# A transformer block on one core: the gate projection spread over the first attention steps, and the last two heads' values behind the first output block

## The chip, the cores and the metric

The kernel runs on one core of a Trainium2 chip. The metric is the device time of one execution in microseconds (us); lower is better. The engines named here are TensorE (PE in the profile), ScalarE (ACT), VectorE (DVE), GpSimd (POOL) and SyncE (SP), whose queue issues the weight loads.

## The reference, cut to what matters

Two transformer blocks run one after the other on 256 tokens of width 1024. The change is in the first one, in its token mixer, between the two feed-forward layers:

```python
h = _rms_norm(x, mix_norm[layer])
proj = h @ w_in[layer]
aq, ak, av, hq, hf, hi, hg = jnp.split(proj, split_at, axis=-1)
...
attn_out = _dilated_attention(aq, ak, av).astype(x.dtype).reshape(b, s, ATTN_WIDTH)
rec = _hgrn2(hq.reshape(b, s, HG_HEADS, HG_EXPAND), hf.reshape(b, s, HG_HEADS, HG_EXPAND),
             hi.reshape(b, s, HG_HEADS, HG_VDIM), lower_bounds[layer]).astype(x.dtype)
rec = _rms_norm(rec, hg_out_norm[layer]) * jax.nn.silu(hg.reshape(b, s, HG_HEADS, HG_VDIM))
mixed = jnp.concatenate([attn_out, rec.reshape(b, s, HG_WIDTH)], axis=-1)
x = x + mixed @ w_out[layer]
```

There are eight attention heads of 64 channels and a chunked linear recurrence of four heads of 128 channels, in chunks of 64 tokens. The gate `hg` is used only at the end: its silu multiplies the normalised output of the recurrence. The value `av` is used from the first head's probabilities on.

## The kernel before, in words

**Weights.** All weights come in blocks of 128 x 2048 floats. A list `plan` gives their order; `sp_stream` loads them into a ring of eight places as places come free. Products are made to float32 precision from halves: `act_split` (L293) has ACT round a block to its high half (the copy at L299), `dve_split` (L302) has DVE subtract it to get the low half (L307), and each product is three matmuls (high by high, high by low, low by high). A high half has one of four places, so block n is split only after block n-4 is used up on PE. A block is held by both engines in the order of their own programs: each `act_split(..., index + SPLIT)` written between other work splits the blocks up to four ahead.

**Order.** Every engine has a program of its own, written out by hand, which runs strictly in order; semaphores join them. PE's program for the mixer is `pe_mix` (L733), ACT's is `act_mix` (L768), DVE's is `dve_mix` (L875). All matmuls are issued by `mm` (L178).

**Projections.** `pe_tok` (L528) multiplies the tokens by a 1024 x 512 weight: two blocks (halves of the contraction), each 24 matmuls of 512 columns, into two PSUM banks (one for each 128 tokens). The blocks are `w_tok` 0 and 1 (q and k), 3 (`hi`), 4 (the gate `hg`) and 2 (`av`), used in this order. Between the two halves of `w_tok` 4 stand the recurrence's first products of heads 0 and 1 (`pe_rec_head`, with transposes at L649), after it those of heads 2 and 3 and the turning of q (`pe_qk_turn`, L699); between the halves of `w_tok` 2 stand the first chunk state (`pe_rec_state`) and the turning of k. ACT empties the banks with `kept` (L797): copies for `hi` and `av`, silu for the gate into `SHG`.

**Attention steps.** Then comes a loop over 11 steps. Step i holds on PE the scores of head i (`pe_scores`, two matmuls with 64 rows of weights), the transposes of head i-2's probabilities (`pe_turn_p`, L720) and the values of head i-3 (`pe_pv`, three matmuls). Steps 0 and 1 also hold the chunk states 1 and 2, step 4 the recurrence's outputs (`pe_rec_out`, 20 products). On DVE a step is the bias and minimum (`biased`, L922 and L924), the scaling by the reciprocal sum (`scaled`, L930 to L933) and, in odd steps from 5 on, the low half of two heads' values (`values`, L938); on ACT two exponentials (`exps`, L808 and L810), the copy of the transposed probabilities (`turned_p`, L817) and the high half of the values (L821). ACT takes the squares of the recurrence's outputs in step 6 (`squares`, L832, eight of them) and their roots in step 8 (L838); DVE makes the means in step 7 (`means`) and the gated product in step 9 (`gated`, L971). `states` (L956) carries the chunk states forward on DVE.

**Output.** Four blocks of `w_out` follow (`pe_down`, 24 matmuls each) into banks 2 to 5: block 0 needs heads 0 to 3, block 1 heads 4 to 7, blocks 2 and 3 the recurrence, whose gated outputs `pe_rec_turn` (L684) transposes between blocks 0 and 1 and `rec_xt` (L843 on ACT) writes back. The next stage is the residual addition and the norm before the second feed-forward layer, and then that layer.

## Time and profile before

| what | us |
|---|---|
| median of three runs | 1333.2 |
| lowest and highest of the three | 1331.91 and 1340.69 |
| the profiled execution, its own time | 1335.28 |
| its span in the trace | 1333.4 |
| busy time of PE over the span, and its share | 1269.5 (95%) |
| busy time of DVE and of ACT | 612.2 (46%) and 466.9 (35%) |
| the token mixer with its output blocks, in the trace | about 214 to 347 |

The page gives for each engine the time in which it was busy, as a share of the span. In the timeline a row is a run of like instructions: its start, the time from the first one's start to the last one's end, the engine, line and operation, how many, and in brackets how long the engine stood idle before it and what released it. The ends of matmuls are modelled and overlap the next one's start, so the time of PE work is best read from start to start. A float32 matmul that isn't made from halves is two instructions in the trace, a transpose is one.

### The profile page before, as it was taken

What the parts mean: (1) busy time and instruction counts of PE and PEld (TensorE: products, weight loads), DVE (VectorE), ACT (ScalarE), POOL (GpSimd) and SP (SyncE); (2) the same over time, 40 slices, a digit from 0 to 9 for tenths busy, and PEclk for the clock granted to TensorE, in tenths of its full rate; (3) what the DMA queues carried; (4) which work ended last, traced back from release to release, by engine and by line L of the source; (5) the groups of instructions that cost most, each with busy time, mean ns of one, the idle gap of its engine ahead of it and who ended that gap; (6) DMA issues with size and microseconds to landing.
All of it is one profiled execution on the core that took longest, in us unless ns stands there. A gap on an engine that the chain in (4) does not pass through costs nothing.

```text
span 1333.4 us, 18498 instructions
## 1 busy us (share of the span) xinstructions
PE 1269.5 (95%) x7906; PEld 924.0 (69%) x7906; DVE 612.2 (46%) x816; ACT 466.9 (35%) x634; POOL 205.6 (15%) x207
## 2 busy tenths in 40 slices
PE   6999999998999999999899999997999899999995
PEld 6999997886799999888664444434898665444432
DVE  6644556845676764476731111117465651111114
ACT  5544344655446444325410101014676420001111
POOL 0000000410499990030000000000033000000000
PEclk9999999999999999989999999998999999999998
DMA  9555553540555555515599999996523399999992
GB/s 390 185 180 180 186 190 129 191 159 28 174 185 187 190 189 167 190 41 188 200 373 419 422 421 420 421 421 248 169 92 127 127 350 395 421 421 421 421 420 113
DMA packets 47750, 338.33 MB, mean 254 GB/s; under 512 B 5296, under 2 KB 5296, under 8 KB 7728
## 3 DMA queue, kind: packets, MB, share of 16 engines
q1 hardware_dynamic: 45936, 330.53, 64.6%
q10 hardware_dynamic: 1728, 6.55, 1.3%
q8 instruction: 66, 1.08, 0.3%
q14 instruction: 20, 0.16, 0.0%
HBM read 336.02 MB, written 1.05 MB: 253 GB/s over the span
## 4 chain that ended last, share of the span: by engine, by line
PE 89%; DVE 7%; ACT 2%; issue 1%; DMA 1%; SPq 0%; ACTq 0%; DVEq 0%
PE pb L178 88%; DVE halves L307 1%; DVE SM L1476 1%; DVE Xs L1487 1%; DMA ring<-in_ffn_w 1%; PE pb L1916 1%; DVE Xs L403 0%; DVE Xs L1482 0%; DVE Xs L405 0%; DVE XN L340 0%; ACT halves L299 0%; DVE p L1655 0%; DVE XN L349 0%; DVE Xs L1500 0%; DVE XTl L392 0%
## 5 line engine op out<-in xcount | busy, mean ns | idle before, releaser
L178 PE MATMUL pb<-XTh,halves 128*128 128x256 f32 x1856 | 338.8, 283 | 6.9 <-DVE XTl L392 4.9
L307 DVE TENSOR_TENSOR halves<-ring,halves 128x2048 fp32r<-128x2048 f32 (+1 forms) x122 | 285.1, 2352 | 130.2 <-ACT halves L299 129.9
L178 PEld LDWEIGHTS pb<-XTh,halves 128*128 128x128 f32 x1856 | 291.2, 192 | 9.1 <-issue 4.1
L178 PE MATMUL pb<-XTl,halves 128*128 128x256 f32 x928 | 262.3, 283 | 0.0
L299 ACT CAST halves<-ring 128x2048 fp32r<-128x2048 f32 (+1 forms) x122 | 227.4, 1874 | 83.4 <-PE pb L178 79.4
L178 PE MATMUL pb<-ring,gather 128*64 128x512 f32 x832 | 189.8, 598 | 3.2 <-DVE gather L2054 1.7
L178 PEld LDWEIGHTS pb<-XTl,halves 128*128 128x128 f32 x928 | 177.8, 192 | 0.9
L178 PE MATMUL pb<-halves,XTh 128*128 128x512 f32 x512 | 160.5, 395 | 5.0 <-DVE halves L307 3.0
L178 PEld LDWEIGHTS pb<-ring,gather 128*64 128x64 f32 x832 | 57.5, 137 | 109.2 <-issue 105.0
L2050 DVE TENSOR_TENSOR slots_h<-slots_silu,pb 128x256 f32<-128x256 f32 x32 | 13.5, 421 | 229.3 <-ACT slots_silu L2012 229.3
L178 PEld LDWEIGHTS pb<-halves,XTh 128*128 128x128 f32 x512 | 95.6, 190 | 26.0 <-DVE halves L307 6.0
L178 PE MATMUL pb<-halves,HTh 128*128 128x512 f32 x352 | 110.8, 396 | 0.0
L178 PE MATMUL pb<-halves,XTl 128*128 128x512 f32 x256 | 100.0, 391 | 0.0
L2058 DVE SCALAR_TENSOR_TENSOR slots_y<-pb,SM,slots_y 128x512 fp32r<-128x512 f32 x32 | 24.0, 751 | 117.4 <-ACT slots_y L2024 117.4
L178 PEld LDWEIGHTS pb<-places,XN 128*128 128x128 f32 x512 | 60.1, 193 | 23.4 <-issue 23.4
L1679 POOL TENSOR_TENSOR p<-p,CO 128x256 f32<-128x256 f32 x16 | 14.9, 959 | 392.1 <-DVE p L1659 392.1
L2024 ACT ACTIVATE slots_y<-pb,SM 128x512 fp32r<-128x512 f32 x32 | 22.0, 688 | 152.2 <-PE pb L178 152.2
L178 PEld LDWEIGHTS pb<-halves,HTh 128*128 128x128 f32 x352 | 64.8, 188 | 14.1
L178 PE MATMUL pb<-ring,slots_ht 128*64 128x512 f32 x320 | 72.9, 597 | 0.0
L178 PE MATMUL pb<-halves,HTl 128*128 128x512 f32 x176 | 69.6, 395 | 0.0
L178 PE MATMUL pb<-places,XN 128*128 128x128 f32 x512 | 65.8, 283 | 1.6 <-ACT gate_sig L1840 1.6
L2016 ACT COPY slots_ht<-pb 128x256 f32<-128x256 f32 x32 | 11.9, 372 | 138.4 <-PE pb L1916 138.0
(348 smaller groups left out, 1389.4 us busy)
## 6 DMA issues: line engine op xcount, KB each, us to landing
ring<-in_moe_w SPq DMA_DIRECT2D x144, 1024.0 KB, 13.6
ring<-in_ffn_w SPq DMA_DIRECT2D x66, 1024.0 KB, 5.0
extra<-in_moe_w SPq DMA_DIRECT2D x48, 1024.0 KB, 14.6
ring<-in_w_tok SPq DMA_DIRECT2D x10, 1024.0 KB, 5.0
ring<-in_ple_gate SPq DMA_DIRECT2D x8, 1024.0 KB, 4.9
ring<-in_w_out SPq DMA_DIRECT2D x4, 1024.0 KB, 4.9
ring<-in_ab_out SPq DMA_DIRECT2D x4, 1024.0 KB, 4.9
ring<-in_sb_v SPq DMA_DIRECT2D x4, 1024.0 KB, 22.8
```

Of the source, the lines that this page charges most:

```text
L178: return e.matmul(out, l, r, start=start, stop=stop, **kw)
L299: e.copy(split_of(n)[0], raw_of(n)).then_inc(*high.mark(n))
L307: e.tensor_tensor(l, raw_of(n), h.bitcast(F32), ALU.subtract).then_inc(*low.mark(n))
L1476: s = e.bn_stats(st4[:, t, h, :], X3[:, t, h * 512:h * 512 + 512])
L1487: e.scalar_tensor_tensor(x, x, r, GB[:, 1024:2048], ALU.mult, ALU.add).then_inc(*x_new.mark("norm", i, t))
L1679: e.tensor_tensor(diag(LL[h % 8]), diag(LL[h % 8]), strict2, ALU.mult).then_inc(*sb_strict.mark(h))
L1916: j = e.transpose(banks[7][:, c * 128:c * 128 + 128], HM[n][:, c * 128:c * 128 + 128], ident)
L2016: e.copy(HT4[p % 2][:, 2 * n:2 * n + 2, :], banks[7][:, 0:256]).then_inc(*s.h_kept.mark(p, n))
L2024: e.activation(Y[h][0], down_bank(p, h)[:, :], ACT.Copy, scale=slot_gate[:, p:p + 1]).then_inc(*s.y_high.mark(p, h))
L2050: e.tensor_tensor(HM[n], SL[n], banks[5 + n][:, 256:512], ALU.mult).then_inc(*s.mul.mark(p, n))
L2058: e.scalar_tensor_tensor(Y[h][1], down_bank(p, h)[:, :], slot_gate[:, p:p + 1], Y[h][0].bitcast(F32), ALU.mult, ALU.subtract).then_inc(*s. ...
```

## The change

The gate's projection (`w_tok` 4) changes places with that of the values (`w_tok` 2), in the plan and in `pe_mix`: values go first, to banks 4 and 5, with the products of heads 0 and 1 and the turning of q between the halves. q is turned into banks 2 and 3 as k is. A new function `pe_gate` issues the gate's 48 matmuls in four pieces, to banks 6 and 7: 8 ahead of state 0, then 13, 13 and 14 at the end of the PE work of steps 0, 1 and 2 (in step 2 ahead of the transposes). The chunk states 1 and 2 move from steps 0 and 1 to steps 1 and 2, and the recurrence's outputs from step 4 to step 3. The values of head 0 and 2 now wait until ACT has emptied banks 6 and 7.

ACT takes the gate's silu, one split and the first four squares in step 3, the last four squares in step 8 and the roots in step 10; a split moves to before step 0 and one to step 1. DVE has splits in steps 0, 1 and 3, and the means and the gated product in steps 9 and 10. The values of heads 6 and 7 move behind output block 0, whose first write to each bank now waits for the last reader of that bank.

```diff
--- before.py
+++ after.py
@@ -209,7 +209,7 @@
         plan_ffn("ffn1", a["ffn1_w13"], a["ffn1_w2"], GROUPS)
         plan_all("w_hf", a["w_hf"])
         plan_all("w_hq", a["w_hq"])
-        for i in (0, 1, 3, 4, 2):
+        for i in (0, 1, 3, 2, 4):
             plan_all(("w_tok", i), a["w_tok"][i])
         plan_all("w_out", a["w_out"])
         plan_ffn("ffn2", a["ffn2_w13"], a["ffn2_w2"], GROUPS)
@@ -632,7 +632,7 @@
         rec_att, rec_state, rec_out, rec_turned = signal("rec_att", mix_pe), signal("rec_state", mix_pe), signal("rec_out", mix_pe), signal("rec_turned", mix_pe)
         qk_turned, att_z, p_turned, att_v = signal("qk_turned", mix_pe), signal("att_z", mix_pe), signal("p_turned", mix_pe), signal("att_v", mix_pe)
 
-        last_tok = index[("w_tok", 2), 1]
+        last_tok = index[("w_tok", 4), 1]
 
         def pe_rec_head(e, h):
             P = banks[h % 2]
@@ -686,13 +686,13 @@
                 i.then_inc(*rec_turned.mark(hp))
 
         def turned_bank(i, gp):
-            return banks[(2 if i else 6) + gp]
+            return banks[2 + gp]
 
         def pe_qk_turn(e, i):
             q3 = qk[i].rearrange("p (t d) -> p t d", t=2)
             e.wait_ge(*roped.at(i, 1))
             for gp in range(2):
-                e.wait_ge(*(tok_kept.at(4, gp) if i else qk_norm.at(1, gp)))
+                e.wait_ge(*(qkt_kept.at(0, gp) if i else q_dec.at(1)))
                 for k in range(2):
                     for t in range(2):
                         g = 2 * gp + k
@@ -724,11 +724,26 @@
             P, p = banks[6 + h // 2 % 2], PT[h % NP]
             o_, hv = slice((h % 2) * 64, (h % 2) * 64 + 64), slice(h * 64, h * 64 + 64)
             e.wait_ge(*pt_kept.at(h))
-            if h >= 4 and h % 2 == 0:
-                e.wait_ge(*mix_low.at("pv", h // 2 - 2))
+            if h % 2 == 0:
+                e.wait_ge(*(tok_kept.at(4, h // 2) if h < 4 else mix_low.at("pv", h // 2 - 2)))
             mm(e, P[o_, 0:128], V3[:, 0, hv], p[:, 0:128], True, True)
             mm(e, P[o_, 128:256], V3[:, 0, hv], p[:, 128:256], True, False)
             mm(e, P[o_, 128:256], V3[:, 1, hv], p[:, 256:384], False, True).then_inc(*att_v.mark(h))
+
+        def pe_gate(e, first, stop):
+            for n in range(first, stop):
+                half, t, k, part = n // 24, n // 12 % 2, n // 3 % 4, n % 3
+                blk, W = index[("w_tok", 4), half], both(split_of(index[("w_tok", 4), half]), lambda x: x.rearrange("p (k n) -> p k n", k=4))
+                if n % 24 == 0:
+                    e.wait_ge(*low.at(blk))
+                if half == 0 and k == 0 and part == 0:
+                    e.wait_ge(*qk_norm.at(1, t))
+                i = mm(e, banks[6 + t][:, :], XT3[part == 2][:, 4 * half + k, t * 128:t * 128 + 128], W[part == 1][:, k, :],
+                       half == 0 and k == 0 and part == 0, half == 1 and k == 3 and part == 2)
+                if n % 24 == 23:
+                    i.then_inc(*used.mark(blk))
+                elif n == 35:
+                    i.then_inc(*half_done.mark(("w_tok", 4)))
 
         def pe_mix(e):
             pe_proj(e, ("w_hf", 0), XT3, banks[0], "mix")
@@ -739,26 +754,30 @@
             pe_tok(e, ("w_tok", 1), 6, 7)
             e.wait_ge(*forget.at(1))
             pe_tok(e, ("w_tok", 3), 0, 1)
-            e.wait_ge(*q_dec.at(1))
-            pe_tok(e, ("w_tok", 4), 2, 3, between=lambda: (pe_rec_head(e, 0), pe_rec_head(e, 1)))
+            e.wait_ge(*qk_norm.at(0, 1))
+            pe_tok(e, ("w_tok", 2), 4, 5, between=lambda: (pe_rec_head(e, 0), pe_rec_head(e, 1), pe_qk_turn(e, 0)))
             pe_rec_head(e, 2)
             pe_rec_head(e, 3)
-            pe_qk_turn(e, 0)
-            e.wait_ge(*qk_norm.at(0, 1))
-            pe_tok(e, ("w_tok", 2), 4, 5, between=lambda: (pe_rec_state(e, 0), pe_qk_turn(e, 1)))
-            for i in range(11):
+            pe_qk_turn(e, 1)
+            pe_gate(e, 0, 8)
+            pe_rec_state(e, 0)
+            for i in range(10):
                 if i < 8:
                     pe_scores(e, i)
-                if i < 2:
-                    pe_rec_state(e, 1 + i)
-                elif i == 4:
+                if i in (1, 2):
+                    pe_rec_state(e, i)
+                elif i == 3:
                     pe_rec_out(e)
+                if i < 3:
+                    pe_gate(e, 8 + 13 * i, 21 + 13 * i if i < 2 else 48)
                 if 2 <= i <= 9:
                     pe_turn_p(e, i - 2)
-                if i >= 3:
+                if 3 <= i < 9:
                     pe_pv(e, i - 3)
             e.wait_ge(*mix_low.at("pv", 1))
-            pe_down(e, "w_out", XT3, range(1), 2)
+            pe_down(e, "w_out", XT3, range(1), 2, free=lambda b: att_max.at(6 + b) if b < 2 else pt_kept.at(4 + b))
+            pe_pv(e, 6)
+            pe_pv(e, 7)
             pe_rec_turn(e)
             e.wait_ge(*mix_low.at("pv", 3))
             pe_down(e, "w_out", XT3, range(1, 2), 2)
@@ -824,14 +843,13 @@
                 e.wait_ge(*att_masked.at(h))
                 e.copy(ksT[:, h * 256:h * 256 + 256], banks[h % 2][:, 256:512]).then_inc(*ks_kept.mark(h))
 
-            def squares():
-                for tt in range(2):
-                    e.wait_ge(*rec_out.at(tt))
-                    for h in range(4):
-                        hv = slice(h * 128, h * 128 + 128)
-                        i = e.activation(XN3[:, tt, hv], banks[1 - tt][:, hv], ACT.Square,
-                                         accum_out=rss[:, 4 * tt + h:4 * tt + h + 1])
-                i.then_inc(*rec_sq.mark())
+            def squares(tt):
+                e.wait_ge(*rec_out.at(tt))
+                for h in range(4):
+                    hv = slice(h * 128, h * 128 + 128)
+                    i = e.activation(XN3[:, tt, hv], banks[1 - tt][:, hv], ACT.Square,
+                                     accum_out=rss[:, 4 * tt + h:4 * tt + h + 1])
+                i.then_inc(*rec_sq.mark(tt))
 
             def roots():
                 e.wait_ge(*rec_mean.at())
@@ -844,30 +862,34 @@
                                  scale=par("hgn")).then_inc(*mix_high.mark("rec", hp))
             act_split(e, c, index[("w_tok", 3), 0] + SPLIT)
             kept(3, 0, HI, ACT.Copy)
-            act_split(e, c, index[("w_tok", 4), 0] + SPLIT)
+            act_split(e, c, index[("w_tok", 2), 0] + SPLIT)
             kept_head(0)
             kept_head(1)
-            kept(4, 2, SHG, ACT.Silu)
+            turned_qk(0, -0.125)
+            kept(2, 4, V, ACT.Copy)
             kept_head(2)
             kept_head(3)
-            turned_qk(0, -0.125)
-            act_split(e, c, index[("w_tok", 2), 0] + SPLIT)
+            turned_qk(1, 1.0)
             e.wait_ge(*rec_state.at(0))
             e.copy(prev[:, 0:512], banks[0][:, :]).then_inc(*state_0.mark())
-            turned_qk(1, 1.0)
-            kept(2, 4, V, ACT.Copy)
+            act_split(e, c, index[("w_tok", 2), 1] + SPLIT)
             for i in range(12):
                 if i < 8:
                     exps(i)
+                if i == 1:
+                    act_split(e, c, index[("w_tok", 4), 0] + SPLIT)
+                elif i == 3:
+                    kept(4, 6, SHG, ACT.Silu)
+                    act_split(e, c, index[("w_tok", 4), 1] + SPLIT)
+                    squares(0)
                 if 2 <= i <= 9:
                     turned_p(i - 2)
                 if i >= 5 and i % 2:
                     values((i - 5) // 2)
-                if i == 6:
-                    squares()
-                elif i == 8:
+                if i == 8:
+                    squares(1)
+                elif i == 10:
                     roots()
-            act_split(e, c, last_tok + SPLIT)
             rec_xt()
             for g in range(3):
                 act_split(e, c, index["w_out", g] + SPLIT)
@@ -958,7 +980,7 @@
                 i.then_inc(*state_n.mark(n))
 
             def means():
-                e.wait_ge(*rec_sq.at())
+                e.wait_ge(*rec_sq.at(1))
                 e.tensor_scalar(rss, rss, 1.0 / 128, 1e-6, ALU.mult, ALU.add).then_inc(*rec_mean.mark())
 
             def gated():
@@ -981,10 +1003,9 @@
             dve_split(e, c, index[("w_tok", 3), 0] + SPLIT)
             masked(0)
             masked(1)
-            dve_split(e, c, index[("w_tok", 4), 0] + SPLIT)
+            dve_split(e, c, index[("w_tok", 2), 0] + SPLIT)
             masked(2)
             masked(3)
-            dve_split(e, c, index[("w_tok", 2), 0] + SPLIT)
             for i in range(12):
                 if i < 8:
                     biased(i)
@@ -992,13 +1013,19 @@
                     scaled(i - 1)
                 if i >= 5 and i % 2:
                     values((i - 5) // 2)
-                if i in (1, 2):
-                    states(i)
-                elif i == 7:
+                if i == 0:
+                    dve_split(e, c, index[("w_tok", 2), 1] + SPLIT)
+                elif i == 1:
+                    states(1)
+                    dve_split(e, c, index[("w_tok", 4), 0] + SPLIT)
+                elif i == 2:
+                    states(2)
+                elif i == 3:
+                    dve_split(e, c, index[("w_tok", 4), 1] + SPLIT)
+                elif i == 9:
                     means()
-                elif i == 9:
+                elif i == 10:
                     gated()
-            dve_split(e, c, last_tok + SPLIT)
             rec_xt()
             for g in range(2):
                 dve_split(e, c, index["w_out", g] + SPLIT)
```

## Rows read from the trace of the kernel before

**Rows 1.** The page: its first line.
```profile
span 1333.4 us, 18498 instructions
```

**Rows 2.** Windows by stage: start and end, then length, busy times, PEclk, DMA share, GB/s.
```profile
270.00:300.00 30.00, 30.00 (x171) 25.41 (x170) 12.18 (x18) 16.57 (x20) 1.89 (x5) 1.00 0.42 145
300.00:327.00 27.00, 23.04 (x139) 15.47 (x137) 13.02 (x66) 15.31 (x62) 0.00 (x0) 0.94 0.09 35
```

**Rows 3.** Timeline of PE, from the third token projection to the recurrence's transposes.
```profile
270.56 0.61 PE L178 MATMUL pb<-halves,XTh 128*128 128x512 f32 x2
...
290.55 1.16 PE L178 MATMUL pb<-p,p 64*128 64x128 f32 x8
291.64 1.09 PE L699 MATMUL pb<-CO,p 128*128 128x128 f32 x8
...
298.13 2.83 PE L178 MATMUL pb<-p,p 64*128 64x128 f32 x28
301.97 0.55 PE L720 MATMUL pb<-CO,p 128*128 128x128 f32 x3 [1.01 <-DVE p L933]
302.44 0.92 PE L178 MATMUL pb<-p,p 64*128 64x128 f32 x4
304.21 0.55 PE L720 MATMUL pb<-CO,p 128*128 128x128 f32 x3 [0.85 <-DVE p L933]
304.92 7.99 PE L178 MATMUL pb<-p,p 128*64 128x128 f32 x50 [0.17 <-ACT p L817]
312.85 0.55 PE L720 MATMUL pb<-CO,p 128*128 128x128 f32 x3
313.32 1.72 PE L178 MATMUL pb<-p,p 128*64 128x128 f32 x10
314.97 0.55 PE L720 MATMUL pb<-CO,p 128*128 128x128 f32 x3
...
320.69 0.55 PE L720 MATMUL pb<-CO,p 128*128 128x128 f32 x3
323.11 1.45 PE L178 MATMUL pb<-p,p 128*64 128x128 f32 x6 [1.88 <-ACT p L817]
324.57 0.90 PE L720 MATMUL pb<-CO,p 128*128 128x128 f32 x3
325.40 1.79 PE L178 MATMUL pb<-p,p 128*64 128x128 f32 x12
```

**Rows 4.** A window of 1 us, PE alone: busy, then its granted clock.
```profile
325.00:326.00 1.00, 1.00 (x6) 0.50 0.00 0
```

**Rows 5.** The chain that ended last, two pieces: start, length, what.
```profile
292.73 5.48 PE pb L178 x24
...
319.75 1.34 ACT XN L832 x11
```

**Rows 6.** Timeline of ACT: two 512-column copies, Exp's table, one step, a split.
```profile
285.12 1.09 ACT L802 ACTIVATE p<-pb 128x512 f32<-128x512 f32 x2
...
298.85 1.28 ACT L808 ACT_TABLE_LOAD   x1
300.14 0.40 ACT L808 ACTIVATE p<-p,SM 128x128 f32<-128x128 f32 x1
...
318.40 0.40 ACT L808 ACTIVATE p<-p,SM 128x128 f32<-128x128 f32 x1 [1.04 <-DVE SM L924]
...
319.30 0.46 ACT L817 COPY p<-pb 128x384 f32<-128x384 f32 x1
...
327.50 1.91 ACT L299 CAST halves<-ring 128x2048 fp32r<-128x2048 f32 x1
```

**Rows 7.** Timeline of DVE: bias to scaling of one step, a split.
```profile
315.08 0.29 DVE L922 CUSTOM_DVE_ANT_0 p<-CO,pb 128x128 f32<-128x128 f32 x1 [7.10 <-PE pb L178]
...
316.03 0.35 DVE L933 TENSOR_SCALAR p<-p,SM 128x256 f32<-128x256 f32 x1
...
329.44 2.29 DVE L307 TENSOR_TENSOR halves<-ring,halves 128x2048 fp32r<-128x2048 f32 x1
```

## The prediction

> **What bounds the kernel now.** I read the page first, for the span of 1333.4 us [rows 1], then windows by stage to find where PE is short of work. Up to 300 us the mixer's PE is never idle, with ACT busy 16.6 and DVE 12.2 of 30 us [rows 2]: PE alone bounds it there. From 300 to 327 us PE has idle time, 27.00 less 23.04 = 3.96 us, and its clock averages 0.94. So at most a few microseconds lie open to this change, and the rest of the span only moves with it. The timeline says where they lie. The transposes of heads 0 and 1 wait 1.01 and 0.85 us for scaled probabilities, the values of head 0 another 0.17, and the values of head 5 wait 1.88 us for ACT's copy: 3.91 us in all [rows 3]. The first three are the start of a pipeline with nothing to fill it: Exp's table is loaded at 298.85 and the first exponential starts at 300.14 [rows 6], while PE has already used up its scores and states. The fourth stands behind ACT's eight squares, which begin at 319.75 in the chain and hold the copy back [rows 5]. Right after it the clock is granted at 0.50, that is 1.2 instead of 2.4 GHz [rows 4], and there the values of a head take 1.46 us (323.11 to 324.57) and three transposes 0.83 (to 325.40), where they otherwise take 0.90 (half of the 1.79 for twelve instructions) and 0.47 (312.85 to 313.32) [rows 3]. That is (1.46 - 0.90) + (0.83 - 0.47) = 0.92 us lost.
>
> **The change part by part.** From 270.56 to 298.13 PE works 27.57 us without a wait [rows 3]. All of that work stays, in another order, but 40 of the 48 gate matmuls leave it. 24 matmuls take 5.48 us, ends included [rows 5], so I use 0.227 each: 40 x 0.227 = 9.1 us. The steps then begin at 289.0 instead of 298.1.
>
> Prices of small work on PE [rows 3]: transposes 0.47; values of a head 0.90; scores 1.65 - 0.90 = 0.75 (the ten instructions from 313.32 to 314.97 are a head's values and scores); the recurrence's outputs, 304.92 to 312.85 less values and scores, 6.28. The first three scores and two states took 2.83 us together. Alone the scores would be 3 x 0.75, and a state between 0.3 (what is left of the 2.83, halved) and 1.09 (state 0, 290.55 to 291.64). The gate pieces break that run up: it now costs between 2.83 and 3 x 0.75 + 2 x 1.09 = 4.43. A score still stands against a state in steps 1 and 2, so I take 0.55 a state, 3.35 in all, a loss of 0.5 (bounds 0 and 1.6).
>
> Steps 0 to 2: 289.0 + 3.35 + 9.1 + 0.47 for head 0's transposes = 301.9, where scores 3 start; before they started at 302.44 [rows 3]. Step 3 with the next scores: 0.75 + 6.28 + 0.47 + 0.90 + 0.75 = 9.15, so the transposes of head 2 begin at 311.1; before 312.85. The start-up waits are gone, 2.03 us less 0.5 for the broken run, rounded: 1.7 us.
>
> What hides them must hold on the other engines. A step of ACT is 0.90 from the first exponential to the copy [rows 6], about 1.3 with it; biased and scaled on DVE take 1.30 (315.08 to 316.38) [rows 7]. Splits are 1.91 on ACT and 2.29 on DVE [rows 6, 7]. In steps 0 to 2 the new order lets ACT wait for the 24th gate matmul, at about 295, to split a block; behind that wait stand exponential 2 and the copy of head 0's transposes, behind the split on DVE stand bias 2 and head 1's scaling. Exponential 1 comes at about 294.7 and scaling 0 at 295.3, 6 us before PE turns them; scaling 1, behind DVE's split, ends at about 301.3, and PE asks for it at 308.9 behind the recurrence's outputs. So nothing reaches PE there.
>
> Step 3 is the tight one. ACT ends exponential 3 at about 304.5. Then come a table load for silu 1.28, two silus 1.09 (as the two 512-column copies), a split 1.91, four squares 1.0 (eight end about 2 us after 319.65), the copy of head 1 0.37 and Exp's table again 1.28: 6.9 us [rows 5, 6], to 311.5. PE meanwhile has the recurrence's outputs to 308.9, transposes, head 0's values and scores 4 to 311.1. Head 1's copy is there at 310.2, and its values are due at 311.6: 1.4 us to spare. Exponential 4 isn't ready to start before about 311.9 for the DVE's bias: 0.4 to spare. DVE's split ends at 311.2, just when scores 4 arrive; scaling 3 ends at about 312.6, and its transposes are due at 313.2: 0.6 to spare. If the cover is short, each microsecond over it is a microsecond on PE. Banks 6 and 7 are empty at about 307, ahead of head 0's values at 309.4.
>
> The second part: the squares are split, four in step 3, four in step 8 behind head 6's copy. The 1.88 us wait goes, and with it, I take it, the fall of the clock, 0.92. What is late next: the last transposes (head 7) wait for scaling 7, which stands behind the values' low half on DVE. Exponential 7 and the scaling come about 0.55 us later than PE asks. Heads 6 and 7's values (1.8 us) now stand behind output block 0, so their ACT copies hide in its 5.44 us; bank 5's reader, head 7's copy, is behind 1.0 us of squares and ends about 0.7 after the transposes, while the block first needs that bank 1.36 us in. The recurrence's transposes need the gated product, done some 2.5 us ahead; output block 1 needs the high and low halves of heads 6 and 7, about 0.9 us after their values, less 0.79 of transposes (1.09 with ends): 0.15 of wait. A split that stood ahead of `rec_xt` is done earlier and was covered anyway.
>
> Sum: 2.03 + 1.88 + 0.92 = 4.83 gone; 0.5 + 0.55 + 0.15 = 1.2 new: 3.6 us shorter. The gate's ring places come free some 10 us later, at about 295 and 301 instead of before 291; their loads are for the second feed-forward layer, whose weights are due after 358, with the DMA engines 42% and 9% busy here [rows 2]: nothing. The table load added for silu in place of the old one and the second load of Exp are in the 6.9 us. The profiled execution, 1335.28 in its own time, would be 1331.7; it lay 2.1 above the median of the runs. From the median, 1333.2 - 3.6 = **1329.6**.
>
> The trace has Exp's first use 1.29 us behind its table load's start, with no pause between [rows 6]. "ScalarE: Activation LUTs" of the Trainium skill (What ACT_TABLE_LOAD costs) says that every switch of set costs a load and a drain, some 2.66 us, and its rules ask for all calls of one set together, which this change undoes. The trace disagrees with the size; by the page's figure the step-3 block would be 2 x 1.38 longer, the second rival's case.
>
> **Rivals.** *More than that (1328.0).* The broken run costs nothing, and waits that the modelled ends hide (298.13 to 333.5 holds some 0.4 us that my prices don't fill) go too: 3.6 + 0.5 + 0.7 at most, so about 1328.4, rounded with the missing 0.4 to 1328.0. For it: only ACT idle of 1 to 2 us is seen before most steps. Against: two alternating chains, DVE to ACT and back, stay as they were.
>
> *ACT's step 3 is over its cover (1331.9).* If the block of 6.9 is 2.8 longer (two switches of 1.28 become about twice that, or the squares wait), of which 0.4 is covered, PE waits about 2.3 us in steps 4 to 6: 3.6 - 2.3 = 1.3 gained. For it: margins of 0.4 to 1.4 us. Against: load and first use lie back to back.
>
> *Slower (1337).* The same place, one mechanism further: PE waits once for about 1.9 us in step 4 or 5, as it did before head 5's values, and its clock falls to 1.2 GHz while five steps of small work are still to come. A step is 0.75 + 0.47 + 0.90 = 2.1 us of PE; at the lower level the rows give 1.46 for 0.90 and 0.83 for 0.47, a factor 1.65, so 1.4 us more a step, 7 for five: -3.6 + 7 = +3.4, about 1336.6. It decides from some 3 low steps on. For it: just one such wait was followed by the fall. Against: before, it came back within some 3 us.
>
> *No difference (1333).* The waits only move: ACT and DVE have their work of steps 3 to 8 in a loop as long as PE's, and the time saved ahead is given back at head 7. For it: the chain runs through ACT ahead of head 5. Against: ACT and DVE were idle up to 7 us before 315.08 [rows 7].
>
> **How the numbers follow.** The forecast 0.50, more gain 0.12, the covered step short 0.18, no difference 0.13, slower 0.07. The range 1326.5 to 1334.5 takes the forecast, both neighbours and no difference, with the bounds 0 and 1.6 of the broken run and about a microsecond of spread of the median; it leaves out the slower case. All cases are far inside 1% (13 us), about what a measurement of this kernel can tell from no change; the runs before spread over 8.8 us. So faster by over 1% 0.03, slower by over 1% 0.03, within 1% 0.94.
>
> **What would show it.** No wait of PE ahead of the transposes of heads 0 and 1; the transposes of head 2 near 311; values of head 5 without a wait and a granted clock of 1.00 through the steps; a short wait at head 7's transposes; ACT with two table loads around two silus and 6.9 us between exponentials 3 and 4; output block 1 starting near 329.9 instead of 333.5. A wait of a microsecond or more in step 4 or 5, or a clock of 0.5 there, would prove it wrong.

## The result, and the profile after

The changed kernel takes 1328.94 us (median of 16 runs, 1325.73 to 1336.33). The kernel before, run beside it as often, takes 1340.25 (1331.23 to 1343.51), not the 1333.2 of its first three runs. The ratio is 0.9929, 95% interval 0.9909 to 0.9948: by the ratio 9.5 us less, by the two medians 11.3. The time of the changed kernel came out near the forecast (1329.6); the time won is more than twice the 3.6 us that I worked out, so most of it needs another explanation.

The runs of before give the first hint: 5 of the 16 lie at 1331 to 1333, 11 at 1339.7 to 1343.5. Over all runs made beside the experiments below and one of its own there are 128 executions of it: 46 up to 1337 us, with median 1332.0, and 82 above, with median 1341.6. Of the changed kernel 27 are known, none above 1337, with median 1328.9. I call these the lower and the upper group. Not all of the 82 are alike: 74 lie at 1339.6 and above, with a mean clock of 0.974 to 0.981 where it is known, and eight at 1337.8 to 1338.3 with 0.982. No trace of one of these eight was taken.

The profiled executions tell only part of it: 1326.9 against 1333.4 us. First the page of after, its first line.

```profile
span 1326.9 us, 18501 instructions
```

The windows by stage, as in [rows 2]:

```profile
270.00:300.00 30.00, 30.00 (x162) 24.93 (x161) 14.69 (x28) 16.39 (x26) 3.32 (x5) 1.00 0.41 138
300.00:327.00 27.00, 26.27 (x155) 18.51 (x155) 14.29 (x57) 18.91 (x58) 0.00 (x0) 1.00 0.15 56
```

PE's idle time between 300 and 327 us went from 3.96 to 0.73 us and the clock stays at 1.00. PE's timeline, as in [rows 3] (the gate's and the output blocks' matmuls are left out):

```profile
277.43 0.61 PE L178 MATMUL pb<-p,p 128*128 128x128 f32 x4
...
289.22 1.81 PE L178 MATMUL pb<-p,p 64*128 64x128 f32 x12
...
294.14 1.81 PE L178 MATMUL pb<-p,p 64*128 64x128 f32 x12
295.88 0.73 PE L178 MATMUL pb<-halves,XTh 128*128 128x512 f32 x2
...
304.15 0.49 PE L720 MATMUL pb<-CO,p 128*128 128x128 f32 x3
304.57 7.19 PE L178 MATMUL pb<-p,p 64*128 64x128 f32 x44
311.69 0.55 PE L720 MATMUL pb<-CO,p 128*128 128x128 f32 x3
312.17 1.72 PE L178 MATMUL pb<-p,p 128*64 128x128 f32 x10
313.82 0.55 PE L720 MATMUL pb<-CO,p 128*128 128x128 f32 x3
...
322.38 0.87 PE L178 MATMUL pb<-p,p 128*64 128x128 f32 x6 [0.17 <-ACT p L836]
323.76 0.55 PE L720 MATMUL pb<-CO,p 128*128 128x128 f32 x3 [0.52 <-DVE p L955]
...
330.81 1.09 PE L684 MATMUL pb<-CO,XN 128*128 128x128 f32 x8
331.80 0.72 PE L178 MATMUL pb<-halves,XTh 128*128 128x512 f32 x2
```

The waits of heads 0 and 1 are gone, head 5's is 0.17 instead of 1.88, head 7's transposes wait 0.52. I measure the mixer from the products of recurrence head 0 to output block 1, since everything ahead is only shifted: 331.80 - 277.43 = 54.37 us, before 333.51 - 276.00 = 57.51. That is 3.14 less.

The rest of the 6.5 us between the two traces lies outside. Ahead of the mixer the after trace is 1.43 us later; its clock was low near 20 us. And in the second block's state-space stage, between the same two hand-overs from ACT and to DVE (560.07 to 625.14 us after, 562.10 to 631.73 before, in the chains), the trace of before is 4.56 us longer. Windows of 10 us there (PE alone: busy, clock), first of before:

```profile
560.00:570.00 10.00, 9.32 (x198) 0.78 0.36 125
570.00:580.00 10.00, 10.00 (x153) 0.54 0.01 2
```

and of after:

```profile
560.00:570.00 10.00, 9.32 (x313) 1.00 0.31 108
570.00:580.00 10.00, 10.00 (x62) 1.00 0.12 29
```

The code there is the same in both kernels; the clock was at 1.2 GHz for most of the stretch in one execution and not in the other. So +1.43 - 3.14 - 4.56 = -6.3 of -6.5, of which only the -3.14 belongs to the changed lines. This fall is a term of its own: the kernel with the waits of the mixer filled, below, has it too (0.62 from 562 to 580 us), and the upper-group trace below does not (1.00). And neither trace is from the upper group. That left two questions: where the upper group's 9 us are, and whether the change took them away or luck did.

### The profile page after: what moved, and what is told of

The parts are those of the page before. It is cut to its first block, busy times and chain, and to the rows that moved or that the text cites. A ratio compares the mean times of both kernels' runs of the same rounds, so it can differ in the third digit from the quotient of the medians.

```text
span 1326.9 us, 18501 instructions
## 1 busy us (share of the span) xinstructions
PE 1264.8 (95%) x7906; PEld 920.4 (69%) x7906; DVE 612.2 (46%) x816; ACT 468.7 (35%) x635; POOL 206.0 (16%) x207
## 4 chain that ended last, share of the span: by engine, by line
PE 89%; DVE 8%; ACT 1%; issue 1%; DMA 1%; SPq 0%; ACTq 0%; DVEq 0%
PE pb L178 87%; DVE halves L307 1%; DVE SM L1503 1%; DVE Xs L1514 1%; DMA ring<-in_ffn_w 1%; PE pb L1943 1%; DVE Xs L403 0%; DVE Xs L1509 0%; DVE Xs L405 0%; DVE XN L340 0%; ACT halves L299 0%; DVE p L1682 0%; PE pb L720 0%; PE pb L364 0%; DVE Xs L1527 0%
## 6 DMA issues: line engine op xcount, KB each, us to landing
ring<-in_moe_w SPq DMA_DIRECT2D x144, 1024.0 KB, 12.7
```

## The experiments

Each kernel was run 6 to 12 times, beside 11 to 35 runs of the kernel before on the same chip. Each has one trace.

**The kernel before once more.** Unchanged.

> The kernel before, once more, for the clock of each of its runs and a second trace. Its sixteen runs lie in two groups, five at 1331 to 1333 and eleven at 1340 to 1344, and the trace shown is of neither (1335.3). Theory A (the clock elsewhere): the upper group has the granted clock fall to 1.2 GHz in a later stage, as the trace of before has from about 567 to 578 us and that of after has not; it has nothing to do with the mixer. Then a trace of the upper group shows the mixer's output block 1 starting about 61.5 us after the start of the third token projection, as before (63.0), and the extra time behind 550 us. Theory B (the clock in the mixer): in the upper group the clock falls already at one of the start-up waits near 302 to 304 us and stays at 1.2 GHz through the recurrence's outputs and steps; then the mixer alone is 5 us or more longer in such a trace. Both expect a mean clock lower by about 0.005 to 0.01 in the upper group.

Measured: median 1340.35, 2 of 12 runs in the lower group, and the trace is from the upper one (1343.39, mean clock 0.976 where the lower group's runs have 0.987). Its windows of 10 us, PE alone:

```profile
300.00:310.00 10.00, 8.14 (x33) 0.68 0.23 94
310.00:320.00 10.00, 10.00 (x40) 0.50 0.00 0
320.00:330.00 10.00, 10.00 (x36) 0.50 0.01 2
330.00:340.00 10.00, 9.91 (x48) 0.79 0.00 1
```

The first two of them in the trace of [rows 3], for comparison:

```profile
300.00:310.00 10.00, 7.97 (x45) 1.00 0.22 92
310.00:320.00 10.00, 9.97 (x68) 1.00 0.00 0
```

The PE timeline of the upper-group trace:

```profile
301.92 0.55 PE L720 MATMUL pb<-CO,p 128*128 128x128 f32 x3 [1.01 <-DVE p L933]
302.40 0.92 PE L178 MATMUL pb<-p,p 64*128 64x128 f32 x4
304.17 0.90 PE L720 MATMUL pb<-CO,p 128*128 128x128 f32 x3 [0.85 <-DVE p L933]
305.00 13.92 PE L178 MATMUL pb<-p,p 128*64 128x128 f32 x50
318.84 0.90 PE L720 MATMUL pb<-CO,p 128*128 128x128 f32 x3
319.68 3.12 PE L178 MATMUL pb<-p,p 128*64 128x128 f32 x10
322.73 0.90 PE L720 MATMUL pb<-CO,p 128*128 128x128 f32 x3
```

The reader should lay this beside [rows 3]. The waits are the same to the hundredth, 1.01 and 0.85 us. But at the second one the transposes already take 0.83 us (304.17 to 305.00) instead of 0.47, and then the 50 instructions behind take 13.9 us instead of 8.0. A step takes 3.89 us (318.84 to 322.73) instead of 2.12, and it stays so for 30.7 us: windows of a quarter of a microsecond have the clock go down near 303.6, inside the second wait, and come back near 334.3, where head 5's values run. The wait for ACT behind the squares has gone, because PE is now the late one. In all the mixer is 67.36 us long instead of 57.51: +9.85, which is the distance between the groups. Theory B of the expectation holds, theory A falls.

**Waits filled, nothing moved.**

```diff
+                if 2 <= i <= 3:
+                    mm(e, banks[7][:, :], ident, CO[:, 0:512], True, True)
                 if 2 <= i <= 9:
                     pe_turn_p(e, i - 2)
+                if i == 8:
+                    e.wait_ge(*att_max.at(6))
+                    for _ in range(2):
+                        mm(e, banks[2][:, :], ident, CO[:, 0:512], True, True)
                 if i >= 3:
```

> The kernel before with float32 matmuls of 512 columns, whose result nobody reads, put where PE waits: one ahead of the transposes of heads 0 and 1 each, two ahead of the values of head 5. No work is moved and ACT and DVE do the same. Theory A: only the 0.9 us of slow clock behind head 5 goes, and the fillers may overrun by some tenths: 0 to -1 us, and the two groups of times stay as common as before. Theory B: the upper group of times is gone, since no idle time is left in the mixer for the clock to fall after: all runs at 1331 to 1334, a median some 7 us lower.

Measured: median 1332.09, all 12 runs between 1330.4 and 1335.0. The useful work on PE stands where it stood; only idle time became matmuls without a use, and 8 us of median are gone. In its trace the transposes of heads 0 and 1 start at 301.95 and 304.24, as in [rows 3], so the useful work was not made earlier:

```profile
304.24 0.50 PE L720 MATMUL pb<-CO,p 128*128 128x128 f32 x3
304.91 7.99 PE L178 MATMUL pb<-p,p 128*64 128x128 f32 x50 [0.17 <-ACT p L823]
...
325.05 1.51 PE L178 MATMUL pb<-p,p 128*64 128x128 f32 x12
```

The mixer is 56.88 long, 0.63 less than in the lower-group trace: that is what the short fall behind head 5 cost it. The median, 1332.09, is that of the lower group, so the fillers took away the long fall and little else. In the upper group the clock of the mixer, not the waits' own length, is the larger cost.

**Only the first two waits filled.**

```diff
+                if 2 <= i <= 3:
+                    mm(e, banks[7][:, :], ident, CO[:, 0:512], True, True)
```

> The kernel before with a float32 matmul of 512 columns ahead of the transposes of head 0 and of head 1 only; the wait of 1.88 us at head 5's values stays. Theory B, now sharpened: the granted clock falls at the waits of heads 0 and 1 in two executions of three and stays at 1.2 GHz through all the small matmuls up to output block 0, which costs some 9 us, so this kernel loses the upper group of times: at most 1 run of 12 above 1337, median 1332 to 1333, and only the short fall behind head 5 is left. Rival C: it is the sum of the waits in the stretch, or the later one, that decides: then the upper group stays in part, with falls that begin at 323 us, and it costs less than 3 us each time. Rival A (nothing to do with the mixer): two thirds of the runs stay at 1338 and more.

Measured: median 1333.81, highest 1337.79; nothing at 1338 or above, against 19 of the 32 runs of before beside it at 1340 and above. Two runs lie at 1337.3 and 1337.8 where I allowed one above 1337, and the median is 0.8 over the range. The trace has the fall only behind the wait of 1.87 us at head 5, and it is short; the mixer is 58.04. So the first waits set off the long fall, the later one a short one. Which of the first two does it, or whether it takes both, no run separates.

**The second part alone.** Squares split, roots later, values of heads 6 and 7 behind output block 0, in the order of before:

```diff
+                if i == 4:
+                    squares(0)
+                elif i == 8:
+                    squares(1)
...
+            pe_down(e, "w_out", XT3, range(1), 2, free=lambda b: ...)
+            pe_pv(e, 6)
+            pe_pv(e, 7)
```

> The kernel before with the second part of the change alone: squares of the first 128 tokens in step 4 and of the others in step 8, roots in step 10, values of heads 6 and 7 behind output block 0; the gate's projection stays where it was. The steps' rows give: the wait of 1.88 us and the slow clock (0.92) go, 0.55 + 0.15 new: -2.1 us against the kernel before's lower group. Theory A: the share of runs in the upper group stays. Theory B, with the fall at the start-up waits of heads 0 and 1, which this kernel keeps: the upper group stays as well; with the fall behind head 5: it goes. A rival: the four squares in step 4 stand ahead of head 2's copy and hold it back by 1 us, then only -1.

Measured: median 1340.79; 7 of 12 in the upper group, as with the kernel before, and the trace is one of them (mixer 66.78). Five are below 1337, four of these at 1326.2 to 1328.3. The part alone leaves the first waits and with them the upper group. These four are some 3 us lower than the 1329.9 that 2.1 us of gain would give, and even a little below the changed kernel; with four such runs and no trace of one I can't say where that comes from.

**The changed kernel with the gate ahead of the steps.** This undoes the spread and nothing else.

```diff
-            pe_gate(e, 0, 8)
+            pe_gate(e, 0, 48)
...
-                if i < 3:
-                    pe_gate(e, 8 + 13 * i, 21 + 13 * i if i < 2 else 48)
```

> The changed kernel with all 48 gate matmuls ahead of state 0, so that steps 0 to 2 have no projection in them; everything else as changed. Theory B: the start-up waits are back (ACT's split and the load of Exp's table now stand ahead of exponential 0, so 2 us or more), the clock falls there in half of the runs or more, and these are 8 us or more above the changed kernel; the runs without a fall 2 to 3 us above it, at 1329.5 to 1331.5. Rival: ACT and DVE are free of their splits earlier and the wait is below 1 us, the clock keeps up, and the kernel is within 1.5 us of the changed one.

Measured: median 1341.87, 10 of 12 at 1340.7 to 1351.7, the two others at 1335.3 and 1335.7. Its trace:

```profile
304.10 0.90 PE L720 MATMUL pb<-CO,p 128*128 128x128 f32 x3 [2.81 <-DVE p L953]
304.93 12.44 PE L178 MATMUL pb<-p,p 64*128 64x128 f32 x44
317.30 0.90 PE L720 MATMUL pb<-CO,p 128*128 128x128 f32 x3
```

One wait of 2.81 us, for a scaling that stands behind ACT's split and table load and DVE's split, and after it the 44 instructions that took 7.1 us take 12.4; the mixer is 69.38 long. The two lowest runs are about 4 us above my range for a run without the fall; they have a mean clock of 0.983, so by that clock a fall of some kind is in them too; no trace shows one of them. Everything that the change brought is gone with this one part of it: the spread is what matters.

**The changed kernel with the squares together in step 6.**

```diff
-                    squares(0)
...
-                if i == 8:
+                if i == 6:
+                    squares(0)
                     squares(1)
```

> The changed kernel with all eight squares in step 6 (roots and gated product where the change has them). No start-up wait, one later wait. By the steps' rows: ACT has 2.0 us of squares behind head 4's copy and the exponential of head 7 waits, as before; PE waits some 1.5 to 1.9 us at head 5's values, while the 1 us less in step 3 helps nobody. Against the changed kernel +1.2 to +2 us in runs where the clock keeps up; if the clock falls there, it lasts only to output block 0, some 5 us of small work, +1 to +3 more, in up to half of the runs. Rival: a fall there lasts as long as the one at the start-up waits (30 us, +8).

Measured: median 1331.64, 12 runs at 1330.4 to 1334.9, so +2.7 against 1328.9. The wait at head 5 is back with 1.88 us, and so is a fall of the clock, from about 323.3 to 326.8:

```profile
322.78 1.03 PE L178 MATMUL pb<-p,p 128*64 128x128 f32 x6 [1.88 <-ACT p L836]
324.17 0.90 PE L720 MATMUL pb<-CO,p 128*128 128x128 f32 x3 [0.36 <-DVE p L955]
```

The mixer is 57.26 - 54.37 = 2.9 us longer. The rival of a 30 us fall is out: the fall ends 2 us into output block 0 in the trace, and no run is above 1334.9.

**The changed kernel without the values behind output block 0.**

```diff
-                if 3 <= i < 9:
+                if i >= 3:
                     pe_pv(e, i - 3)
...
-            pe_pv(e, 6)
-            pe_pv(e, 7)
```

> The changed kernel with the values of heads 6 and 7 back in steps 9 and 10 ahead of output block 0; all else as changed. My forecast gave this move nothing of its own: it costs 0.15 at output block 1. If the steps run as forecast, head 7's values would follow its transposes by about 1.4 us (the squares and the copy on ACT), of which head 6's values cover 0.9: +0.5 to +1.3 us against the changed kernel. Theory B: with such a wait the clock could fall again, then +1.5 to +2. A rival: ACT's squares of step 8 are late and all of the gain of this part is in the hiding: +2 or more.

Measured: median 1329.35 (+0.4, just under the +0.5 to +1.3 expected), mixer 54.67 (+0.30), no run in the upper group. The hiding of these copies is the smallest part.

**The second part with filled waits.** The kernel of "the second part alone" with the two fillers of "only the first two waits filled".

> The kernel before with the second part of the change (squares split, values of heads 6 and 7 behind output block 0) and one float32 matmul of 512 columns ahead of the transposes of heads 0 and 1; the gate's projection stays whole and where it was. Theory B: this has the whole effect of the change on the clock and lacks only what the spread fills with work, the waits of 1.01, 0.85 and 0.17 us less the 0.5 of the broken run: no run above 1337, and 1 to 2 us above the changed kernel, a median of 1329.5 to 1331. Rival: the spread itself keeps the clock up in later stages too, then this one is 3 us or more above the changed kernel.

Measured: median 1331.41, 1326.6 to 1337.9, in the trace a mixer of 54.83 us and no slow clock in it. Two runs are at 1337.1 and 1337.9, so "none above 1337" was missed, as in the kernel with the first waits filled; nothing lies at 1338 or more. The median is 0.4 over its range and 2.5 above the changed kernel's beside it (1328.92), of which the mixers of the two traces explain 0.46. Four of the twelve runs are above 1333, with mean clocks of 0.981 and 0.983. No trace shows where their clock is low, so the rival, that the spread keeps the clock up in later stages too, is not ruled out for these 2 us. With the clock taken care of, real work in place of the fillers brought only 0.46 us of mixer. That was the surprise that led to the last two kernels: the waits filled were worth 2 us.

**The changed kernel again, beside it.** Unchanged.

> The changed kernel once more, beside the one above on the same chip, for a direct comparison: median 1328 to 1330 as in its sixteen runs, up to 3 of 12 runs at 1333 to 1336.5, none above 1337. In its trace, as in the first one, the mixer from the start of the third projection to the recurrence's transposes takes 58.8 us, and any run above 1333 has its slow clock in a later stage.

Measured: median 1328.92, 11 runs at 1327.4 to 1335.2, the mixer 54.36 long, 54.37 in the first trace. The kernel of the fillers in the state-space stage, which has the same mixer, has 54.37 as well, so a mixer's length without a fall repeats to 0.01 us. The ratio, 0.9939 (0.9911 to 0.9967), agrees with the first.

**Fillers in the state-space stage**, in the changed kernel:

```diff
+            mm(e, banks[3][:, :], ident, CO[:, 0:512], True, True)
             pe_proj(e, ("ab_u", 0), XT3, banks[0], "ssm")
             pe_proj(e, ("ab_u", 1), XT3, banks[1])
+            mm(e, banks[3][:, :], ident, CO[:, 0:512], True, True)
             pe_inputs(e)
```

> The changed kernel with one float32 matmul of 512 columns ahead of each of two waits at the start of the second block's state-space stage (the wait for the first low half of the transposed tokens near 547, and the 0.68 us wait for ACT near 560 us). The changed kernel's sixteen runs hold three above 1333; theory: in them the clock falls behind these waits, near 565, and stays low through 10 us of matmuls of 64 columns, as in the trace shown of the kernel before, +4.5 to +7. Then no run above 1332 here, and the median within 0.5 us of the changed kernel (each filler takes about 0.9 us in a wait of 0.7 to 0.9). Rival: the fall comes from the small matmuls themselves, not from the wait ahead: as many runs above 1333 as before.

Measured: median 1328.94, 9 runs at 1326.1 to 1332.0. None is above 1333, where the changed kernel has 4 of 27; with nine runs that would happen about once in four times by luck alone. It is inconclusive, and no gain shows in the median.

**States 1 and 2 back in steps 0 and 1**, in the changed kernel:

```diff
-                if i in (1, 2):
-                    pe_rec_state(e, i)
+                if i < 2:
+                    pe_rec_state(e, 1 + i)
```

> The changed kernel with chunk states 1 and 2 back in steps 0 and 1 (behind scores 0 and 1), the outputs and all else as changed. In the trace of after each run of a head's scores and a state takes 1.74 us from start to start, where before all of three scores and two states took 2.83. Theory D: what differs is the rows that follow each other: scores of head h and state n use rows 0 to 63 when h or n is even and rows 64 to 127 when it is odd, as the slices say; before, scores 0 stood against state 1 and scores 1 against state 2 (different rows), in the changed kernel scores 1 against state 1 and scores 2 against state 2 (the same rows), and only different rows overlap. Then the two runs take about 1.0 to 1.2 us each instead of 1.74: the mixer from head 0's products to output block 1 at 52.9 to 53.4 us instead of 54.37, and the kernel 1 to 1.5 us faster than changed, a median of 1327.4 to 1328. Rival: the runs are slow because projection matmuls stand on both sides and the pipeline has to change over; then no difference in the mixer's length.

Measured: median 1327.07 (6 runs, 1326.0 to 1329.6), ratio to before 0.9913 (0.988 to 0.9946). The mixer is 53.15 long, 1.22 less than 54.37. Its PE timeline:

```profile
287.78 2.16 PE L178 MATMUL pb<-p,p 64*128 64x128 f32 x20
...
293.05 1.17 PE L178 MATMUL pb<-p,p 64*128 64x128 f32 x12
...
297.33 0.92 PE L178 MATMUL pb<-p,p 64*128 64x128 f32 x4
```

The run of 12 (scores 1 and state 2) is 1.17 us long, where scores 1 and state 1 were 1.81. It has projection matmuls on both sides here too, which rules the rival out. The pairing decides. By the run times alone it would not be shown: this ratio's interval overlaps that of the changed kernel.

**And DVE's low half of values later**, on top of that:

```diff
-                if i >= 5 and i % 2:
+                if i >= 5 and i % 2 and i != 7:
                     values((i - 5) // 2)
+                elif i == 8:
+                    values(1)
```

> The kernel above, and DVE's low half of the values of heads 2 and 3 put behind head 7's scaling (step 8) instead of ahead of it. In the trace of after the scaling of head 7 starts at 322.97, though its exponential ended at 321.96, since DVE stands at the low half until ACT has the high one, and PE waits 0.52 us for it. Theory: the wait goes, 0.4 to 0.5 us on top of the kernel above. Rival: PE is then held by ACT's copy of head 7 or by output block 0's wait for those values, and nothing is gained.

Measured: median 1326.31 (6 runs, 1324.1 to 1328.7), ratio to before 0.9903 (0.987 to 0.9936); the mixer is 52.56, another 0.59 less. The rows that the expectation rested on, of the changed kernel's DVE:

```profile
322.62 0.42 DVE L960 TENSOR_TENSOR XTl<-pb,XTh 128x256 fp32r<-128x256 f32 x1 [1.02 <-ACT XTh L840]
322.97 0.15 DVE L952 RECIPROCAL SM<-SM 128x2 f32<-128x2 f32 x1
```

and the transposes of head 7 in this kernel, which no longer wait:

```profile
321.02 0.87 PE L178 MATMUL pb<-p,p 128*64 128x128 f32 x6 [0.17 <-ACT p L836]
321.82 0.55 PE L720 MATMUL pb<-CO,p 128*128 128x128 f32 x3
```

This last kernel is better than both that the study began with: 1326.3 against 1328.9 and 1340.3. Six runs on another chip don't separate it from the changed kernel by themselves; the mixer lengths (52.56, 54.37, 57.51 or about 67) do.

## Why the prediction was right or wrong, point by point

**The time of the changed kernel** was right: 1329.6 forecast, 1328.9 measured. In part this is luck. The anchor was the median of three runs, and two of them happened to be of the lower group, which holds about one run in three. With two of the upper group, the same sum would have given about 1336.7 (1340.3 - 3.6). And of the sum's two parts one was too large and the other too small, as told below.

**The time won was forecast too small, and the step that failed is the anchor.** "From the median, 1333.2 - 3.6" took three runs, two of them of the lower group, as what the kernel before takes. It holds for the lower group: 1332.0 - 1328.9 = 3.1. But two executions of three were of the other group, and there the change takes away 12.7 us (1341.6 - 1328.9), of which 9.85 are the clock in the mixer, by the one traced pair. The table ahead had the sign of it: 1340.69 beside 1331.91 and 1333.2. I read that as spread.

**The clock term was priced from one execution.** I gave the fall 0.92 us, at head 5. In that trace it cost 0.63, by the kernel with all waits filled. The 0.36 for the transposes was right. The 0.56 for head 5's values was not lost: with the waits filled, these values and a wait of 0.59 us for head 7's transposes together take the same 1.46 us (323.11 to 324.57). And the sum left out the run of twelve from 325.40, which began at 1.2 GHz too [rows 4]: 1.79 against 1.51 with the waits filled, 0.28. The "slower" rival had the mechanism, a wait and then small work at 1.2 GHz through the steps, and a price of 1.4 us a step (1.77 measured), but I put it into the changed kernel, ahead of five steps, and argued "before, it came back within some 3 us". It belonged to the kernel before, at its first waits, with the recurrence's outputs and all the steps behind them. The three kernels with fillers and the one with the gate ahead show this: filled, none of 36 runs is at 1338 or above (four are above 1337), against 79 of the 128 of before; with the gate ahead, whose trace has a wait of 2.81 us, ten of twelve are above 1340.

**Start-up waits gone, 2.03 us:** right. **The broken run, 0.5 (bounds 0 and 1.6):** mis-sized. The two runs of scores and a state take 1.74 us each (294.14 to 295.88) where I had 0.75 + 0.55 = 1.30, together 0.9 more. The pieces of the gate take some 0.2 more each than 0.227 a matmul. Counting from the products of head 0, the transposes of head 2 came 0.46 us earlier than before (313.82 - 277.43 = 36.39 against 312.85 - 276.00 = 36.85), not the 1.7 of the text or the 2.03 - 0.5 = 1.5 of the sum. So of the waits' 2.03 us three quarters were paid back. My sentence "a score still stands against a state" missed which one: the kernel with states 1 and 2 put back shows that the pairing costs 1.22 us.

**The second part, 1.88 + 0.92 less 0.55 + 0.15 = 2.1:** measured 3.14 - 0.46 = 2.7. The wait at head 7's transposes, 0.52, came as forecast, but it was no new one. The kernel with all waits filled, in the old order, has 0.59 us there; in the trace of before it lay hidden under the slow clock, so nothing was to be subtracted. The 1.88 did all go but 0.17: 1.71, with 0.63 for the clock and 0.30 for the values behind output block 0, make 2.64 of the 2.7.

**ACT's step 3:** its length was right to the tenth. It began at 307.20, not 304.5, and 1.43 of that lies ahead of the mixer. Its rows:

```profile
307.20 1.28 ACT L816 ACT_TABLE_LOAD   x1
308.49 1.09 ACT L816 ACTIVATE p<-pb 128x512 f32<-128x512 f32 x2
309.46 1.90 ACT L299 CAST halves<-ring 128x2048 fp32r<-128x2048 f32 x1
...
312.27 0.51 ACT L836 COPY p<-pb 128x384 f32<-128x384 f32 x1
312.80 1.28 ACT L827 ACT_TABLE_LOAD   x1
314.60 0.40 ACT L827 ACTIVATE p<-p,SM 128x128 f32<-128x128 f32 x1 [0.52 <-DVE SM L946]
```

From 307.20 to 314.08, where the second load ends, are 6.88 us (6.9 forecast), and ACT then idles 0.52 for DVE's bias (0.4 forecast to spare). The silus start 1.29 us after their load's start, and the load itself 0.01 us after exponential 3 ends (307.19): by this trace a switch of tables costs the load and nothing ahead of it or behind it, as the exponentials' row of before had said. The Trainium skill's "ScalarE: Activation LUTs" (What ACT_TABLE_LOAD costs) states 2.66 us for it; the trace disagrees. The rival built on the larger size did not come about.

**What stays open.** Why the same two waits, 1.01 and 0.85 us, are followed by the fall in two executions of three and not in the third; whether the falls in the state-space stage follow from the waits ahead of them (no trace of the changed kernel has one, though 4 of its 27 times lie above 1333); the eight times at 1337.8 to 1338.3; where the kernel with the second part and fillers loses its further 2 us; and the low times of the second part alone.

## What to carry to other kernels

Look at all times of the kernel before, and at the mean clock of each, ahead of any sum from one trace: two groups of times are two profiles, and a forecast needs the trace of each. A short wait of TensorE ahead of a long stretch of small matmuls is priced at what the stretch takes at 1.2 GHz, times how often it happens; useless matmuls in the wait tell whether it is so. Real work in their place brought 0.46 us more here, and 1.68 (54.83 - 53.15) once the chunk states were back in their order. When small matmuls with 64 rows are reordered, keep neighbours on different rows.

## What the runs showed of the hardware that I had not expected

In one execution of a kernel the granted clock went from 1.00 to 0.50 inside the second of two waits, of 1.01 and 0.85 us with 1.4 us of work between them, and stayed there for 30.7 us; in another, with the same two waits, it stayed at 1.00. Through nearly the whole stretch of small matmuls the clock did not come back, though the profile shows no wait of PE in it. The same small matmuls held it at 1.00 where it was up: in the trace of after it is 1.00 through all the steps. So a fall at the head of such a stretch costs far more than one at its end, where output block 0 follows: 9.85 us against 0.63 in the trace of before and 1.16 (58.04 - 56.88) in the one with only the first waits filled.

Small float32 matmuls with 64 rows of weights that stand next to each other ran into one another when their rows differed: scores 1 and state 2 (rows 64 to 127, then 0 to 63) 1.17 us, scores 1 and state 1 (the same rows) 1.81, with equal instruction counts. The Trainium skill, "TensorE: Matmul & The Clock Gate", Part 3, states that weight loads overlap running matmuls only where the row groups differ; the trace agrees.
